# Rotary embedding: fp32 permutation matmuls on TensorE replaced by a VectorE partition shuffle

## The reference

```python
def _rope(x, pos):
    """Partial rotary on the first ROT_DIM dims of each head. x (N, T, heads, HEAD_DIM), pos (T,)."""
    inv = 1.0 / (ROPE_THETA ** (jnp.arange(0, ROT_DIM, 2, dtype=jnp.float32) / ROT_DIM))
    ang = pos.astype(jnp.float32)[:, None] * inv[None, :]
    cos = jnp.cos(ang)[:, None, :]
    sin = jnp.sin(ang)[:, None, :]
    half = ROT_DIM // 2
    xr = x[..., :ROT_DIM].astype(jnp.float32)
    x1, x2 = xr[..., :half], xr[..., half:]
    rot = jnp.concatenate([x1 * cos - x2 * sin, x2 * cos + x1 * sin], axis=-1)
    return jnp.concatenate([rot.astype(x.dtype), x[..., ROT_DIM:]], axis=-1)
```

## Time and profile before

| | us |
|---|---|
| median of 3 runs | 2673.03 |
| lowest, highest run | 2672.75, 2674.61 |
| span of the profiled execution | 2671.8 |
| busy in it: TensorE | 2464.1 |
| VectorE | 1352.7 |
| GpSimd | 772.3 |
| ScalarE | 528.5 |

### The profile page before, as it was taken

One profiled execution on the slowest core, in us unless ns is written; L12 is line 12 of the kernel. 1 busy time (PEld: TensorE's weight loads), 2 busy tenths in 40 slices (PEclk: granted clock), 3 DMA queues, 4 the chain that ended last, 5 costly groups with the idle time before them and its releaser, 6 DMA issues.

```text
span 2671.8 us, 37036 instructions
## 1 busy us (share of the span) xinstructions
PE 2464.1 (92%) x14763; PEld 2360.2 (88%) x14763; DVE 1352.7 (51%) x1227; ACT 528.5 (20%) x914; POOL 772.3 (29%) x400
## 2 busy tenths in 40 slices
PE   3899995699999999999989989889999999999996
PEld 2888884699999999999979967679999999999996
DVE  2688887534444444344464656644444433444444
ACT  2432221421011110111030057612111011011113
POOL 0132321332333333333322223322333333333320
PEclk9898987799999999999999979988999999999998
DMA  5010100111111111111111020011111111111111
GB/s 162 24 32 16 31 16 8 40 40 40 48 47 47 40 47 47 47 47 47 40 39 40 16 60 1 9 32 40 40 48 47 47 41 45 47 47 47 41 38 70
DMA packets 156781, 110.93 MB, mean 42 GB/s; under 512 B 6487, under 2 KB 142055, under 8 KB 156599
## 3 DMA queue, kind: packets, MB, share of 16 engines
q1 hardware_dynamic: 154352, 98.90, 14.4%
q10 hardware_dynamic: 2371, 11.21, 1.4%
HBM read 105.20 MB, written 8.10 MB: 42 GB/s over the span
## 4 chain that ended last, share of the span: by engine, by line
PE 82%; DVE 9%; ACT 3%; issue 3%; DMA 1%; ACTq 1%; DVEq 0%; POOL 0%
PE PS L1398 53%; PE PS L1416 15%; PE PS L1501 5%; DVE CONV L778 2%; PE PS L1289 2%; PE PS L1450 2%; PE PS L1320 2%; PE PS L1292 1%; DVE X L693 1%; ACT WK L1147 1%; DVE WK L874 1%; DMA WK<-in_state_ffn 1%; PE PS L1557 1%; PE PS L1523 1%; DVE WK L666 1%
## 5 line engine op out<-in xcount | busy, mean ns | idle before, releaser
L1398 PE MATMUL PS<-H,W 128*128 128x344 f32 x9504 | 1531.3, 323 | 47.6 <-DVE H L854 21.9
L1398 PEld LDWEIGHTS PS<-H,W 128*128 128x128 f32 x9504 | 1518.0, 190 | 54.4 <-issue 34.2
L450 POOL CAST W<-RAW 128x1024 fp32r<-128x1024 f32 x176 | 195.2, 1109 | 1580.1 <-issue 782.1
L1416 PE MATMUL PS<-MID,W 128*128 128x344 f32 x3168 | 513.7, 322 | 20.4 <-DVE X L693 10.5
L1416 PEld LDWEIGHTS PS<-MID,W 128*128 128x128 f32 x3168 | 504.5, 190 | 27.0 <-DVE X L693 16.5
L452 POOL TENSOR_TENSOR W<-RAW,W 128x1024 fp32r<-128x1024 f32 x176 | 477.8, 2715 | 14.1
L693 DVE TENSOR_TENSOR X<-PS,X 128x1032 f32<-128x1032 f32 (+1 forms) x184 | 226.2, 1230 | 231.2 <-PE PS L1416 183.4
L778 DVE SCALAR_TENSOR_TENSOR CONV<-WK,PAR,CONV 128x1024 f32 (+1 forms) x152 | 223.9, 1473 | 18.0 <-DVE CONV L778 2.0
L898 DVE TENSOR_TENSOR WK<-PS,WK 128x1032 f32<-128x1032 f32 x44 | 54.3, 1233 | 299.9 <-PE PS L1398 297.6
L1154 ACT ACTIVATE MID<-WK 128x1032 fp32r<-128x1032 f32 x44 | 47.1, 1070 | 678.2 <-DVE WK L900 678.2
L874 DVE TENSOR_TENSOR WK<-PS,WK 128x1032 f32<-128x1032 f32 x44 | 54.3, 1233 | 224.0 <-PE PS L1398 223.9
(11 more groups left out here) (173 smaller groups left out, 1547.8 us busy)
## 6 DMA issues: line engine op xcount, KB each, us to landing
RAW<-in_ffn_w_in SPq DMA_DIRECT2D x176, 256.0 KB, 3.9
RAW<-in_ffn_w_down SPq DMA_DIRECT2D x88, 256.0 KB, 3.8
RAW<-in_conv_w_pw SPq DMA_DIRECT2D x48, 256.0 KB, 4.0
RAW<-in_attn_w_qkv SPq DMA_DIRECT2D x24, 256.0 KB, 3.8
XIN<-in_x_prompt ACTq DMA_DIRECT2D x8, 512.0 KB, 13.2
RAW<-in_attn_w_o SPq DMA_DIRECT2D x32, 128.0 KB, 2.8
out_y_prompt<-YOUT SPq DMA_DIRECT2D x8, 512.0 KB
WK<-in_const_rope ACTq DMA_DIRECT2D x1, 1032.0 KB, 5.3
```

The source lines that it names most:

```text
L450: nc.gpsimd.tensor_copy(W[:, slot, 0, :], RAW[:, slot, :]).then_inc(s_hi, hi.up())
L1398: last = matmul(PS[:, 3 * side + c, 0:CH], W[:, slot, wp, k * P:(k + 1) * P], H[:, hp, k, c * CH:(c + 1) * CH], start=(k == 0 and q == 0), ...
L1416: last = matmul(PS[:, 3 * side + c, 0:CH], W[:, slot, wp, t * BANK + m * P:t * BANK + (m + 1) * P], MID[:, t, hp, c * CH:(c + 1) * CH], st ...
```

## The change

The permutation matmuls and the copies ahead of them are gone. VectorE's `turn_heads` now reads a tile straight from its PSUM side: it multiplies it by the cosines into T1, then shuffles the partitions of the same PSUM side into R with one `stream_shuffle`, which applies one list of 32 partners (`PARTNER`: rows 0 to 7 and 8 to 15 exchanged, the rest in place) inside each group of 32 partitions, then multiplies R by the sines in place, and adds. The shuffle is what releases the PSUM side. The 12 dense tiles of TensorE alternate the sides, the eight query tiles in a loop of four turns in place of the written-out order. Each tile counts once in `s_mm` and `s_pr` instead of twice, and ScalarE's counts follow. The permutation matrix stays among the constants, unused.

```diff
--- before.py
+++ after.py
@@ -329,6 +329,7 @@
 
         UNITS = [(n, p, hf) for n in range(NB) for p in range(2) for hf in range(2)]
         HEADS, KV_READY = 2 + 2 * KT, 5
+        PARTNER = [(i + ROT // 2) % ROT if i < ROT else i for i in range(32)]
         ROW_DMAS = 20
         STORES = 23
         block = ctx.enter_context(nc.Block())
@@ -928,24 +929,18 @@
             v.tensor_tensor(SIN, SIN, RS, ALU.mult).then_inc(s_v, own.up())
             dve.wait_ge(s_v, own.at())
 
-            def raw_heads(s, t):
+            def turn_heads(s, t):
+
+                R = WK[:, 1 + t % 2, 0:T]
+                T1 = WK[:, 3, 0:T]
                 dve.wait_ge(s_mm, mm.next())
                 if heads.due():
                     dve.wait_ge(s_heads, heads.at())
-                v.tensor_copy(chunks(WK[:, 1 + t % 2, 0:T]), side(s)).then_inc(s_pr, pr.up())
-
-            def turn_heads(s, t):
-
-                R = WK[:, 1 + t % 2, 0:T]
-                T1 = WK[:, 3, 0:T]
-                if heads.due():
-                    dve.wait_ge(s_heads, heads.at())
+                v.tensor_tensor(chunks(T1), side(s), chunks(COS), ALU.mult).then_inc(s_v, own.up())
+                v.stream_shuffle(chunks(R), side(s), PARTNER).then_inc(s_pr, pr.up())
                 dve.wait_ge(s_pr, pr.at())
-                v.tensor_tensor(T1, R, COS, ALU.mult).then_inc(s_v, own.up())
-                dve.wait_ge(s_mm, mm.next())
+                v.tensor_tensor(R, R, SIN, ALU.mult).then_inc(s_v, own.up())
                 dve.wait_ge(s_v, own.at())
-                v.tensor_tensor(chunks(R), side(s), chunks(SIN), ALU.mult).then_inc(s_pr, pr.up())
-                dve.wait_ge(s_pr, pr.at())
                 if t < 2:
                     v.tensor_tensor(WK[:, K_TILE[t], 0:T], T1, R, ALU.add).then_inc(s_heads, heads.up())
                     return
@@ -956,14 +951,8 @@
                     src = slice(o * HD, (o + 1) * HD)
                     v.tensor_tensor(QA[rows, j // 2, 2 * (q % 2) + o, :], T1[src, :], R[src, :], ALU.add).then_inc(s_heads, heads.up())
 
-            raw_heads(0, 0)
-            raw_heads(1, 1)
-            for t in range(KT):
-                turn_heads(0, t)
-                if t == KT - 1:
-                    turn_heads(0, KT)
-                raw_heads(1, t)
-            turn_heads(1, KT + 1)
+            for t in range(2 + KT):
+                turn_heads(t % 2, t)
             assert heads.n == HEADS
 
             attention_dve(dve)
@@ -1170,7 +1159,7 @@
             roots()
 
             kvh = Count()
-            act.wait_ge(s_mm, pr.n + 5 + 2 * KT)
+            act.wait_ge(s_mm, pr.n + 4 + KT)
             act.wait_ge(s_heads, 2)
             for p in range(2):
                 F_(KR[:, 0, p, P:PADK], WK[:, K_TILE[p], 0:T], ACT.Copy).then_inc(s_kvh, kvh.up())
@@ -1222,7 +1211,7 @@
             qt = QA[:, :, :, :].rearrange("p a g n -> p (a g) n")
             with turns(act, 0, KT, {hh: 1}) as m:
                 F_(htile(0, m), tile(qt, m), ACT.Copy).then_inc(s_hh, hh.up())
-            pr.n += 12 + KT + 2
+            pr.n += 4 + KT
             residual(R_FFN + 1)
             ffn(1)
 
@@ -1549,26 +1538,13 @@
             ffn()
 
 
-            def swap(side, t):
-                begin_group()
-                raw_group = t + 2 if t < 2 else 2 * t + 1 + (t > KT)
-                pe.wait_ge(s_pr, before + raw_group + 1)
-                for c in range(NCH):
-                    last = matmul(PS[:, 3 * side + c, 0:CH], PERM, WK[:, 1 + t % 2, c * CH:(c + 1) * CH],
-                                  start=True, stop=True)
-                last.then_inc(s_mm, mm.up())
-            before = pr.n
             dense(0, 0, wait_h=True, hooks={2: token_sums})
             dense(1, 1, hooks={1: broadcast, 4: broadcast_samples})
             dense(0, 0)
             dense(1, 1)
-            for t in range(KT):
-                swap(0, t)
-                if t < KT - 1:
-                    dense(1, t % 2)
-                else:
-                    dense(1, t % 2, hooks={1: lambda: swap(0, KT)})
-            swap(1, KT + 1)
+            with turns(pe, 0, KT // 2, {w: 2, started: 2, mm: 2, pr: 2}):
+                dense(0, 0)
+                dense(1, 1)
 
             attention_pe(pe, transpose, PASSES, pr)
 
```

## The result

The changed kernel takes 2652.72 us (median of 4 runs, 2650.73 to 2653.93); the kernel before, run beside it, takes 2672.89 (4 runs, 2669.36 to 2674.61). The ratio is 0.9925, with an interval of 0.9911 to 0.9939: 20.2 us less, where 16.15 were forecast. The time lies 1.3 us under the low end of the range. The profiled span went from 2671.8 to 2649.5 us, 22.3 less.

The account below looks back on a forecast made before the run. TensorE, busy 92% of the span, was taken as the bound. Saving 15.4 us in the dense stretch plus 0.75 us in the tail took 2671.8 to 2655.65 us, or 2656.9 with the runs' 1.2 us offset; range 2654.0 to 2661.5.

Parts of the forecast that it names:

- The dense stretch: TensorE's eight query tiles: without nine swaps they run back to back, 106.36 us becoming 90.94, saving 15.4 us.
- VectorE's turn: VectorE's work per rotary tile: again about 8.3 us, hidden under the next dense tile's 11.37 us.
- The shuffle: VectorE's shuffle out of PSUM: 1.23 us like the copy it replaces, plus 0.1 us for its list of partners.
- The tail: VectorE's path behind the last dense tile to the last sum: 7.17 us becomes 6.4, saving 0.75 us.
- The sum: Whole kernel: 15.4 us from the dense tiles plus 0.75 us behind them, 16.15 us saved.
- TensorE's clock: Start of attention: return to full clock one unit later costs 3.9 us; slightly earlier gains under 1 us.
- The scatter: Whole kernel: executions of the old kernel differ by 1.9 us, 2672.75 to 2674.61.
- The rule on the clock: TensorE's clock: free-running activity window, so the 16 us shift gives every later return a new place, on either side.
- (a): Dense stretch: VectorE becomes the bound; a 6.60 us shuffle gives 2665.3 us, loss from 7.4 us; chance 0.05.
- (b): Attention: TensorE's clock stays low through further units, 3.9 us each, 2660.8 us for one; chance beyond one unit 0.05.
- (c): Dense tiles: saved time returns as another wait, pace stays at 13.08 us, 2672.3 us in all; chance 0.04.
- Theory 1: Follow-up reading: the change is worth 16.3 us; the rest is TensorE's clock falling and returning elsewhere when work moves.

Follow-up runs that it names:

- the warm: Idle matmuls where TensorE stands still ahead of attention: 12 in the old kernel, 2667.76 us; 14 in the changed kernel, 2656.30 us.
- the filled pair: Old and changed kernel, each with idle matmuls in nearly all waits of TensorE: 2642.83 us and 2630.96 us.
- the idle swaps: Changed kernel with nine unread swaps of three matmuls put back on TensorE, VectorE still shuffling: 2672.70 us, ratio 0.9997.
- b_late1: Old kernel with one idle memset (0.66 us) added on VectorE's path at the start of attention: 2665.25 us, ratio 0.9977.
- a_again: Changed kernel, unedited, run again for a second trace: 2650.33 us, ratio 0.9927; the traced execution took 2665.75 us.
- a_late4: Changed kernel with four idle memsets added on VectorE's path behind the last sum: 2657.45 us.
- a_late1: Changed kernel with one idle memset added on VectorE's path at the start of attention: 2653.66 us.
- a_late6: Changed kernel with six idle memsets added on VectorE's path behind the last sum: 2656.62 us.
- b_fill: Old kernel with idle matmuls in nearly all waits of TensorE: 2642.83 us, ratio 0.9893.
- b_warm: Old kernel with 12 idle matmuls where TensorE stands still ahead of attention: 2667.76 us, ratio 0.999.

## Why the prediction was right and wrong

- **The dense stretch**: 15.4 us forecast, 15.40 measured, in this pair and in the warm and the filled pair alike; undone to the hundredth by the idle swaps. Eight tiles take 90.95 us, forecast 90.94.
- **VectorE's turn**: 8.3 us forecast, 7.5 measured. The surcharge beside GpSimd did move to the sine product, but as 1.2 us (2.46 for 1.24) instead of 1.88. It was hidden as said, with 3.9 us to spare.
- **The shuffle**: 1.33 us forecast with its set-up, 1.31 to 1.34 measured with 0.014 us for the list. The estimate from the Trainium skill, page VectorE: DVE Perf Modes, section on the perf-mode tier table, was 1.2 us; the trace is within 0.14 of it.
- **The tail**: sums forecast to end at E + 6.4 and measured at E + 6.28; first score forecast at 14.1 and measured at 14.02; 0.89 us saved for 0.75. The second part of the value transposes starts 2.54 us behind E (2.7) and stays hidden. GpSimd's subtraction ends 1456.36 - 1452.46 = 3.9 us behind the tile (4.2).
- **The sum**: 16.15 us forecast for the change's own work; 16.29 measured. This part needs no correction.
- **The step that failed is the one on TensorE's clock.** It bounded an earlier return at under 1 us. Measured in the profiled pair, the return came 7.6 us sooner behind the first score (17.1 for 24.7) and was worth 3.39 us by the second heads; over the whole span the rest was 6.0 us in that pair and about 4 in the medians (20.2 and 20.3 less 16.3). Two assumptions made the bound too small. The return was tied to the heads matmuls, since the earlier trace rows show it there once; it came behind one group of transposes instead. And the cost was read as one unit or none, for one place, while three later stretches each took a new value too. The late side was given 3.9 us; with as much on the early side the low end would have been 2656.9 - 3.9 = 2653.0 ahead of any scatter and 2651.1 with the 1.9 us. The ends as stated don't come out of their terms, by a little: 2656.9 + 4.4 is 2661.3, and 2656.9 less 0.3, 1.9 and 1 is 2653.7; the measured 2652.72 is below that as well.
- **The scatter** was taken as 1.9 us from three runs. With 15 to 23 runs on a chip, before spans 7 to 11 us.
- **The rule on the clock**: the Trainium skill, page TensorE: Matmul & The Clock Gate, Part 1, has the activity window free-running, so that the point of the change depends on where in it the work falls. The prediction used this for its late side alone. b_late1 (6.7 us faster with work added) and a_again (the same program, another return) are in keeping with the rule; no run here shows the window itself.
- **The rivals**: (a) did not happen at 1.33 us and does with six shuffles, more sharply than worked out, since the sums' 2.48 us were held fixed while GpSimd moves with the dense tile. (b) did not occur: in no traced run did the return come more than 25.3 us behind the first score (a_again, just past the 25 us that the prediction had named). (c) fell: no dense tile waits.

What stays open: why the return comes where it does. Theory 1 gave the sizes for b_late1 and a_late4 and missed those of a_late1, a_late6, the trace of a_again and both pairs with idle matmuls. A part of the 4 us can be chance (theory 2): two sets of runs of after give the same 20 us, but by the intervals of their ratios the gain is 16.3 to 23.8 and 16.0 to 22.7 us, which just reach the 16.3. The most that the runs bear out is this: the change is worth 16.3 us, and the clock took up to 4.8 us from that or added up to 3.9 in the three settings tried (11.5, 11.9 and 20.2 us).

## What to carry to other kernels

Where one engine carries the chain without a gap, work taken from it comes back in full, if the engine that takes it over has idle time within the same period: count the period, not the sum, and let the neighbours that contend with it move too. Any shift of the work also moves the places where TensorE's clock falls and returns; give a forecast the size of one unit at the low clock on either side, and take the scatter from more than three runs. Where a kernel has short waits of TensorE spread over it, idle matmuls in them were worth some 21 us in the changed kernel and 29 in the old one, more than this change; in a single gap they were worth 3 us in one kernel and cost 6 in the other.

## What had not been expected of the hardware

- A busy TensorE can lose its clock: in b_fill it fell while scores ran one behind the other. In b_warm it fell in a wait of 2.36 us, behind 7.91 us of idle matmuls and four groups of scores at 2.4 GHz, and was back 13.7 us later.
- More work can go with less time: 0.66 us added on VectorE's path, and the kernel 6.7 us faster.
- One program can have the clock back at two places: 17.1 and 25.3 us behind the first score in two executions of the changed kernel.
- Two VectorE instructions of the same shape, both inputs in SBUF, differ by what GpSimd does: 1.24 us for the sine product alone, 2.46 beside a subtraction of 2.41; the two sums 2.48 alone and 5.27 beside one, which is itself stretched to 3.24.
- A shuffle of 128 x 1032 fp32 out of PSUM takes 1.33 us, the copy of the same shape 1.23.
